# Three scalings on GpSimd, and latent attention's entrance, copies and end rearranged

## The reference

```python
# layer 0: differential attention, per block of 128 queries
p = softmax(where(causal, q @ k.T * scale, NEG_INF))      # two maps, c = 0 and 1
a = p[:, :, 0] - lam * p[:, :, 1]
o = rms_norm(a @ v, subln) * (1.0 - lambda_init)          # per head, width 128
y = o.reshape(B, S, H * 2 * dh) @ w_o
# layer 1: latent attention
lat = h @ w_in                                            # 384 + 256 + 32 columns
q = (rms_norm(cq) @ w_uq); kv = (rms_norm(ckv) @ w_ukv)   # normalised per head, rotated
p = softmax(where(causal, s, NEG_INF))
y = (p @ v).reshape(B, S, H * MLA_V) @ w_o
```

## Time and profile before

| | us |
|---|---|
| runs shown | 1137.25, 1137.52, 1135.13 (median 1137.25) |
| profiled execution: its own time | 1136.97 |
| its span, first to last instruction | 1135.2 |
| PE busy | 1043.2 (92%) |
| DVE busy | 608.2 (54%) |
| ACT busy | 329.0 (29%) |
| POOL busy | 92.1 (8%) |

### The profile page before, as it was taken

How to read it: one execution, slowest core, us unless ns; L and a number is a source line. 1 busy time by engine, 2 the same in 40 slices (tenths; PEclk the granted TensorE clock), 3 DMA queues, 4 the chain that set the end, 5 groups by cost and what they waited for, 6 DMA issues and landing times.

```text
span 1135.2 us, 15295 instructions
## 1 busy us (share of the span) xinstructions
PE 1043.2 (92%) x5662; PEld 633.0 (56%) x5662; DVE 608.2 (54%) x1460; ACT 329.0 (29%) x896; POOL 92.1 (8%) x129
## 2 busy tenths in 40 slices
PE   4999999999998999897889999999998999979996
PEld 3444444656466666564556556655456656646652
DVE  6899989898646322221246577766235622222224
ACT  4321112875131111111124545666122121111110
POOL 1000000000011111111000000000000111201200
PEclk9999999999999999999999999999998999999999
DMA  9929868928568999999996300401826899999998
GB/s 368 405 79 392 332 259 328 420 83 347 190 270 340 409 417 419 418 418 420 417 396 261 124 1 38 149 1 61 334 88 259 311 420 420 418 414 418 419 416 351
DMA packets 66814, 341.44 MB, mean 301 GB/s; under 512 B 11110, under 2 KB 11366, under 8 KB 36400
## 3 DMA queue, kind: packets, MB, share of 16 engines
q1 hardware_dynamic: 49952, 297.68, 64.8%
q0 software_dynamic: 15120, 37.63, 8.5%
q10 hardware_dynamic: 1664, 5.09, 1.1%
HBM read 320.90 MB, written 37.24 MB: 315 GB/s over the span
## 4 chain that ended last, share of the span: by engine, by line
PE 75%; DMA 8%; SPq 5%; DVE 5%; ACT 3%; issue 3%; DVEq 0%; ACTq 0%; POOLq 0%
PE PP L928 16%; PE PP L694 12%; PE PP L804 10%; PE PP L943 8%; PE PP L716 3%; SPq L531 3%; DMA AHS<-in_moe_w 3%; PE PP L1145 3%; PE PP L667 2%; PE PP L1111 2%; PE PP L1149 2%; PE PP L901 2%; PE PP L753 2%; SPq L547 2%; PE PP L764 2%
## 5 line engine op out<-in xcount | busy, mean ns | idle before, releaser
L694 PE MATMUL PP<-ring,AHS 128*128 128x512 f32 x320 | 139.9, 592 | 0.0
L2028 DVE TENSOR_TENSOR PS<-PS,PP 128x256 f32<-128x256 f32 x33 | 13.9, 421 | 195.9 <-PE PP L928 186.3
L804 PE MATMUL PP<-ring,AHS 128*128 128x512 f32 x256 | 111.4, 593 | 0.8 <-ACT AHS L1491 0.8
L2035 DVE SCALAR_TENSOR_TENSOR PS<-PP,small,GF 128x512 f32<-128x512 f32 x66 | 46.5, 746 | 111.3 <-PE PP L943 100.7
L694 PEld LDWEIGHTS PP<-ring,AHS 128*128 128x128 f32 x320 | 59.7, 190 | 69.8 <-issue 69.8
L928 PE MATMUL PP<-RQK,RV 128*64 128x256 f32 x640 | 75.2, 392 | 10.5 <-issue 8.4
L804 PEld LDWEIGHTS PP<-ring,AHS 128*128 128x128 f32 x256 | 48.0, 190 | 58.4 <-issue 58.4
L928 PE MATMUL PP<-ring,RV 128*64 128x256 f32 (+1 forms) x608 | 75.5, 389 | 4.3 <-ACT RV L1525 1.7
L1549 ACT ACTIVATE PS<-PP 128x256 f32<-128x256 f32 x33 | 12.7, 384 | 217.1 <-PE PP L928 151.1
L928 PEld LDWEIGHTS PP<-RQK,RV 128*64 128x64 f32 x640 | 56.4, 142 | 32.1 <-issue 17.7
L928 PE MATMUL PP<-AHS,RV 128*64 128x256 f32 x640 | 71.9, 380 | 2.1 <-issue 2.1
(11 more groups left out here) (351 smaller groups left out, 1675.4 us busy)
## 6 DMA issues: line engine op xcount, KB each, us to landing
AHS<-in_moe_w SPq DMA_DIRECT2D x61, 1024.0 KB
ring<-in_moe_w SPq DMA_DIRECT2D x58, 1024.0 KB, 21.2
RQK<-in_moe_w SPq DMA_DIRECT2D x52, 1024.0 KB
ring<-in_ada_t SPq DMA_DIRECT2D x22, 1024.0 KB, 19.9
AHS<-in_ada_t SPq DMA_DIRECT2D x18, 1024.0 KB
X<-in_moe_w SPq DMA_DIRECT2D x16, 1024.0 KB, 23.3
ring<-in_da_w_qkv SPq DMA_DIRECT2D x10, 1024.0 KB, 13.8
RQK<-in_ada_t SPq DMA_DIRECT2D x8, 1024.0 KB
```

The source lines that it names most:

```text
L694: last = mm(PB[qkv_bank(n)][:, :], HT[:, c, t * P:(t + 1) * P], us[c // 4][:, (c % 4) * NH:(c % 4 + 1) * NH], start=c == 0, stop=c == C - 1)
L804: last = mm(PB[2 * t + n][:, :], (OT, OTM)[l][:, k, t * P:(t + 1) * P], us[k // 2][:, (k % 2) * D + n * NH:(k % 2) * D + (n + 1) * NH], st ...
L2035: last = stt(ysb[b][:, cols], PB[5 + m][:, :], weight, GF[:, cols], ALU.mult, ALU.mult)
```

## The change

1. Differential attention: `SCALED` is gone. The outputs of tiles 0, 1 and 2 are scaled by GpSimd, in its program behind the zero fill of y_d and the load of a row. Tile 3 stays with VectorE, which first waits for GpSimd's three.
2. Latent attention: the copy of a tile 0 (both heads) goes from ScalarE to VectorE.
3. Entrance: the scores of steps 0 and 1 are made in banks 6 and 7 behind projection 14, with maxima, exponentials and normalisation beside projection 15. The last two transposes of queries and keys use banks 6 and 7. Of the last but one ScalarE copies both. Three groups of fillers (6 + 3 + 8 calls) are left out. The probabilities lie in other places.
4. End: for tile 0, chunks 0 to 2 of the first half of the output projection are put before the transposes of steps 29 and 31 and after the latter, and four more chunks and seven of the second half behind the values of pair 7.

```diff
-def mla_on_vector(i):
+def by_vector_alone(i):
+    return i % T == 0
+def by_both(i):
     return i % T >= 2
...
-        prm = [view(PS, 1024 * b, 2, S) for b in range(3)] + [view(RA, 2560 + T * ROPE, 2, S)]
+        prm = [view(PS, 2048, 2, S), view(RA, 2560 + T * ROPE, 2, S), view(PS, 1024, 2, S), view(PS, 0, 2, S)]
+        prm_first = view(RA, 2560 + T * ROPE + 2 * S, 2, P)
...
@@ tensor, project_out
-                        begun = 1 if (l, t, n) == (0, 0, 0) else 0
+                        begun = 0 if t else C - 1 if l else 1 - n
@@ tensor, mla
+                def scores_ahead(t):
+                    for a in range(2):
+                        o = early_scores(t, a)
+                        mm(o, mq[0][0:QK, a, t * P:(t + 1) * P], mk[0][0:QK, a, 0:(t + 1) * P], start=True, stop=False)
+                        last = mm(o[:, t * P:(t + 1) * P], identb[:, :], maskb[:, :], start=False, stop=True)
+                    last.then_inc(sem("sc"), 1)
...
                     if i >= T:
                         mla_values(i // T - 1, i % T)
+                    if i == 29:
+                        pe.wait_ge(sem("exp"), 32 + 31)
+                        mixed(1, 0, 0, wo, (0,))
+                    if i == 31:
+                        mixed(1, 0, 0, wo, (1,))
                     mla_turn(i)
...
                     if n >= 2:
                         turn_qk(n - 2)
-                first_scores(0)
-                keep_busy(7, 6)
-                turn_qk(4 * T - 2)
-                first_scores(1)
-                turn_qk(4 * T - 1)
-                keep_busy(7, 3)
-                pe.wait_ge(sem("mtev"), 4 * T)
-                pe.wait_ge(sem("mtevD"), 4 * T)
-                for i in range(32):
+                    if n == 4 * T - 2:
+                        scores_ahead(0)
+                        scores_ahead(1)
+                pe.wait_ge(sem("exp"), 32 + 2)
+                turn_qk(4 * T - 2, 6)
+                scores_behind_projection(2, 4 * T - 2)
+                pe.wait_ge(sem("mtev"), 4 * T - 2)
+                pe.wait_ge(sem("mtevD"), 4 * T - 2)
+                attend(0)
+                scores_behind_projection(3, 4 * T - 1)
+                pe.wait_ge(sem("mtev"), 4 * T - 1)
+                turn_qk(4 * T - 1, 6)
+                attend(1)
+                for i in range(2, 32):
...
-                    if i == 2:
-                        keep_busy(7, 8)
-                    if i:
+                    if i > 2:
                         attend(i - 1)
                 attend(31)
+                mixed(1, 0, 0, wo, (2,))
                 for k in range(T):
                     mla_values(7, k)
+                mixed(1, 0, 0, wo, (3, 4, 5))
+                pe.wait_ge(sem("omla"), 7)
+                mixed(1, 0, 0, wo, (6,))
+                mixed(1, 0, 1, wo, range(C - 1))
@@ scalar, mla
+                    if n == 4 * T - 1:
+                        queries_out(n - 2)
                     roots(n)
-                    if n >= 2:
+                    if 2 <= n < 4 * T - 1:
                         queries_out(n - 2)
+                    if n == 4 * T - 2:
+                        exps(1, 0, 0)
+                        exps(1, 1, 1)
                 queries_out(4 * T - 2)
-                exps(1, 0, 0)
+                exps(1, 2, 0)
                 queries_out(4 * T - 1)
-                exps(1, 1, 1)
+                exps(1, 3, 1)
@@ vector, da_attention and output_norm
-                    if i in SCALED:
-                        output_scaled(*SCALED[i])
...
+                dve.wait_ge(sem("on"), T - 1)
                 for half in range(2):
                     output_scaled(T - 1, half)
@@ vector, mla
+                    if by_vector_alone(i):
+                        v.tensor_copy(turned_pair(t), PP[2][:, :, 0:(t + 1) * P].rearrange("p a (k q) -> p a k q", k=t + 1)).then_inc(
                             sem("tev1"), 1)
...
+                    if n == 4 * T - 2:
+                        maxima(1, 0, 0)
+                        maxima(1, 1, 1)
                     heads(n)
-                keys_out(4 * T - 2)
-                maxima(1, 0, 0)
-                keys_out(4 * T - 1)
-                maxima(1, 1, 1)
-                for i in range(32):
+                    if n == 4 * T - 2:
+                        normalise(0)
+                        normalise(1)
+                maxima(1, 2, 0)
+                probabilities_out(0)
+                maxima(1, 3, 1)
+                for i in range(2, 32):
                     normalise(i)
+                    if i == 2:
+                        keys_out(4 * T - 1)
@@ gpsimd, layer 0, behind gate_row(0, 1)
+                    for t in range(T - 1):
+                        pool.wait_ge(sem("osd"), t + 1)
+                        for half in range(2):
+                            ot = OTOK[:, t, half * NH:(half + 1) * NH].rearrange("p (h x) -> p h x", h=4)
+                            factor = hrs[:, 0, 8 * t + 4 * half:8 * t + 4 * half + 4].unsqueeze(2).broadcast_to([P, 4, P])
+                            last = g.tensor_tensor(ot, ot, factor, ALU.mult)
+                        last.then_inc(sem("on"), 1)
```

More of the change, by code:

```diff
@@ L126, with vector_copies, scalar_copies @@
 SUMS = {17: (0, 0), 18: (0, 1), 19: (1, 0), 20: (1, 1), 25: (2, 0), 26: (2, 1)}
-SCALED = {21: (0, 0), 22: (0, 1), 23: (1, 0), 24: (1, 1), 29: (2, 0), 30: (2, 1)}
 ROOTS = {20: 0, 22: 1, 28: 2}
-def mla_on_vector(i):
+def by_vector_alone(i):
+    return i % T == 0
+def by_both(i):
     return i % T >= 2
-def mla_copies(i):
-    return sum(mla_on_vector(j) for j in range(i + 1))
+def vector_copies(i):
+    return sum(by_vector_alone(j) or by_both(j) for j in range(i + 1))
+def scalar_copies(i):
+    return sum(not by_vector_alone(j) for j in range(i + 1))
 def wait(eng, sem, value):
@@ L1151, in project, with turn_qk, scores_behind_projection @@
                     last.then_inc(sem("mla_kv"), 1)
[L1153 removed]
+                def turn_qk(n, bank=4):
                     pe.wait_ge(sem("my"), n + 1)
[L1156 to L1157 removed]
+                    if bank == 4:
+                        wait(pe, sem("mtev"), n)
+                        wait(pe, sem("mtevD"), n)
                     for m, y in enumerate((QY, KY)):
                         for h in range(4):
[L1160 removed]
+                            last = nc.tensor.transpose(PB[bank + m][0:QK, h * P:(h + 1) * P], y[n % 2][:, h, :], ident[:, :])
                     last.then_inc(sem("mt"), 1)
[L1163 to L1165 removed]
+                def scores_ahead(t):
[4 more added lines that the diff above has]
+                    last.then_inc(sem("sc"), 1)
+                def scores_behind_projection(i, n):
                     for name in ("msq", "mev"):
                         pe.wait_ge(sem(name), n + 1)
[L1168 to L1171, removed]
+                    scores(1, i, i % 2)
                 def attend(i):
@@ L1184, in mla @@
                         turn_qk(n - 2)
-                first_scores(0)
-                keep_busy(7, 6)
-                turn_qk(4 * T - 2)
-                first_scores(1)
-                turn_qk(4 * T - 1)
-                keep_busy(7, 3)
-                pe.wait_ge(sem("mtev"), 4 * T)
-                pe.wait_ge(sem("mtevD"), 4 * T)
-                for i in range(32):
+                    if n == 4 * T - 2:
[12 more added lines that the diff above has]
+                for i in range(2, 32):
+                    if i == 5:
+                        pe.wait_ge(sem("mtev"), 4 * T)
+                        pe.wait_ge(sem("mtevD"), 4 * T - 1)
+                    if i == 30:
+                        wo = [take(1, "wo", u) for u in range(4)]
+                        pe.wait_ge(sem("omla"), 6)
                     if i + 2 < 32:
@@ L1348, in exps @@
                     total = ls[:, b, a:a + 1] if l or a else l1[:, DA_H * t + g:DA_H * t + g + 1]
-                    last = fn(dst[:, a, 0:L], PB[2 * pair + a][:, 0:L], ACT.Exp, bias=nmx[:, b, a:a + 1], accum_out=total)
+                    dst = probabilities(i, a) if l else pr[b][:, a, 0:L]
+                    src = early_scores(i, a) if l and i < 2 else PB[2 * pair + a][:, 0:L]
+                    last = fn(dst, src, ACT.Exp, bias=nmx[:, b, a:a + 1], accum_out=total)
                 last.then_inc(sem("exp"), 1)
@@ L1773, in maxima @@
                 wait(dve, sem("exp"), n - 1)
-                red(nmx[:, b], PP[pair][:, :, 0:L], AX.X, ALU.max, negate=True).then_inc(sem("nm"), 1)
+                o = PP[pair][:, :, 0:L]
+                if l and i < 2:
+                    o = PB[6 + i][:, 0:2 * L].rearrange("p (a n) -> p a n", a=2)
+                red(nmx[:, b], o, AX.X, ALU.max, negate=True).then_inc(sem("nm"), 1)
             def da_attention():
```

50 lines of the change are left out of this document (31 added, 19 removed).

## The result

The changed kernel takes 1127.14 us (median of 4 runs, 1126.80 to 1128.31), the one before 1136.97 on the same chip (4 runs, 1135.13 to 1137.52): a ratio of 0.9926 [0.9902, 0.9951]. Forecast were 1128.0 and 1125.8 to 1132.5. The profiled execution took 1127.12, its span is 1125.4. A repeat of both kernels on another chip (last experiment) gave 1128.73 against 1134.40, a ratio of 0.9951 [0.9937, 0.9964]: a gain of 5.7 us there, in place of 9.8 here.

The account below looks back on a forecast made before the run. TensorE was taken to bound three quarters of the chain, with DMA and its queue most of the rest. The terms 0.4 + 2.3 + 3.6 + 2.9 = 9.2 us off gave 1128.0 us, range 1125.8 to 1132.5.

Parts of the forecast that it names:

- What bounds it, and gains pass one to one: Whole kernel: three quarters of the chain is TensorE, and attention ending N us earlier makes the end N us earlier.
- Rival C: Start of layer 1's stream: bound to something that doesn't move, so only 0.4 us stays, 1136.8; chance 0.03.
- Part 1: Differential attention: moving scaling from VectorE to GpSimd gains 0.4 us, between +1.0 and -1.7.
- the choice between the bounds: Differential attention: GpSimd slows VectorE not at all, or VectorE stands for each of four multiplies; 0.4 us gain taken.
- the 1.3 I put in: Differential attention: assumed length in us of one GpSimd 128x512 multiply, the middle of 0.3 and 2.3.
- rival B: Differential attention, steps 21 to 25: L1785 stands behind GpSimd's multiplies, costing 1.0 to 1.7 us, 1129.8; chance 0.12.
- The 0.8 that I gave to an undisturbed VectorE: Differential attention, transposes of steps 22 to 25: gains of 0.27, 0.40 and 0.12 us without VectorE's scaling, together 0.8.
- Part 2: Latent attention's steady groups: tile 0's copy on VectorE removes six gaps of 0.39 us before tile 1's transposes, 2.3 us.
- Part 3: Latent attention's entrance: the reordered schedule starts scores 7 3.7 us earlier; 3.6 us taken, between 1.5 and 4.4.
- Rival A: Latent attention's entrance: without fillers, idle pieces and short transposes let the clock fall, costing 3.5 us, 1131.5; chance 0.11.
- Rival D: Latent attention: clock stays at 1.2 GHz throughout; 15 us of full-clock work affected give 1143; chance 0.04.
- Part 4: End of latent attention: output-projection chunks fill TensorE's idle places, gaining 2.9 us, from below 1.5.

Follow-up runs that it names:

- The delay of 8.04 us: 36 matmul calls whose result nobody reads, put ahead of latent attention's output projection in the changed kernel: 1134.72 us (12 runs).
- the pieces: The changed kernel with each 128x512 multiply of GpSimd cut into four of 128x128, one for each head: 1126.41 us, ratio 0.9927.

## Why the prediction was right, and which step was not

- **What bounds it, and gains pass one to one:** right, within what was measured. The delay of 8.04 us came through as 7.1 in the medians, give or take 2 to 3, and the stages show 7.4 of it ahead of the experts and none returned behind. Rival C (1136.8) is refuted. What the prediction lacked is that an edit can change a stage far behind it (below).
- **Part 1, "I take a gain of 0.4":** wrong in sign, -0.2 measured. Two steps failed. The first is the choice between the bounds: the rival's mechanism is real. L1785's successor stood until the end of the running multiplies in two of the five steps, 0.74 and 0.75 us each. By the Trainium skill (SBUF — State Buffer, "SBUF: two separate sides"), where of a VectorE operation with two SBUF inputs and a GpSimd one that reads SBUF the later waits for the whole of the earlier, this is what had to come, and the traces agree (1.36 and 1.50 us in place of 0.62 and 0.75, and 1.49 in place of 1.04 for the multiply that came second). I had named that rule and weighed it with half, where the row that it spoke of was the very operation that the transposes wait for. The second is the price: a multiply takes 1.02, not the 1.3 I put in, and only two pairs collided with the critical operation where the stage waits for it, so the loss was 0.2 and not the 1.0 to 1.7 of rival B. (The third pair held L1843 for 0.82 us too, at 259.87, but TensorE's steps behind step 25 are not longer for it.) The 0.8 that I gave to an undisturbed VectorE was too low: the pieces show 1.16 in those steps and 1.44 in the stage, and with the multiplies moved away the same steps lose 1.16 as well.
- **Part 2, 2.3:** measured 2.56, a group 10.32 us where 10.36 was forecast. The handovers of 0.04 around the gap went as well. The copy of tile 1 was indeed next and didn't wait: 61.92 of 61.92.
- **Part 3, 3.6:** measured 3.41, of which 0.44 is the removed wait of part 2 in this place. The order laid out by hand was right to 0.12 at the last scores (3.58 against 3.7). The prediction didn't say that part 3 gives nothing without part 2 (+0.53 alone, -2.97 behind it), though its own schedule had VectorE's copy in it.
- **Rival A, the clock at the entrance:** it did not decide here (1.00 in 22.08 us), but its reason holds. Where TensorE stood 2.47 or 2.08 us at this place the clock fell, and once it fell with the unchanged 1.11 and 0.31. A chance of 0.11 for it fits one of seven profiles, as far as seven can say; the price was 1.7 us there and not 3.5. Rival D found no sign: where the clock had fallen in this entrance, the next scores of 512 columns, 3.4 us later, took their 1.88 again.
- **Part 4, 2.9:** measured 2.97, with chunks in the three places forecast. The number holds the 0.94 that part 2 takes by itself: behind parts 2 and 3 the filled end adds 2.00. Parts 2 and 4 were booked right in sum and not each.
- **Sum:** the parts make 0.2 - 2.56 - 3.41 - 2.97 = -8.74 against -9.2. The rest of the -9.85 between the two profiled executions is in stages with no edit in them, -1.08, +0.14, -1.96, -0.14 and +1.95 (the last 0.02 are rounding). The forecast's 1128.0 is so close to 1127.14 because the parts gave 0.46 less than forecast, and the others, each up to 2 us, happened to sum up to 1.09 more. That is luck, and the repeat shows it: there the gain is 5.7 us [4.1, 7.1], which doesn't reach the forecast 9.2, though both profiles of the kernel after have the same edited stages. The kernel before took 1134.13 to 1135.34 (medians) on the three chips of the experiments, 1.6 to 2.8 us less than in the first comparison. So the edited stages bear the prediction out, and the whole gain only in part.

**The stage that grew.** Before, TensorE runs at 0.93 in the 50 us of layer 1's experts from 985.90, and at 0.86 in the matching 50 us of the kernel after. The chain of the kernel after has one long row there, behind the tile of leftover tokens:
```profile
1008.48 6.45 issue
1014.93 6.16 PE PP L946 x33
```
The kernel before has 0.65 us at this place:
```profile
1020.55 0.65 issue
1021.20 8.81 PE PP L928 x64
```
Eight of the fourteen profiles have 6.25 to 7.8 us here, six have 0.65. Those with the long wait take 249.85 to 253.8 us from the first expert step to the end (the median of the eight is 251.4), those with the short one 248.6 to 250.1 (249.6). Both profiles of the kernel after have the long one, but so has the kernel of before without fillers, and the kernel with pieces and fillers has the short one.

It is no chance, though: it goes with the number of matmuls in TensorE's program. The page of each of the eight profiles with the long wait counts 5628 of them, those of the other six 5638, 5662 or 5700. Two pairs of kernels differ by fillers of the entrance alone, some 290 us ahead (in the second pair a semaphore wait comes with them). The kernel before has the 0.65 above; without its 17 fillers it has
```profile
1019.07 6.25 issue
```
and its experts of layer 1 take 249.85 us in place of 249.31. The kernel with the multiplies in pieces has
```profile
1007.44 6.27 issue
```
and with five fillers added it has
```profile
1007.95 0.65 issue
```
with 249.92 us in place of 251.32. So part 3, which leaves out 17 fillers, brought the long wait into the kernel after. In the 20 us from the wait's begin the granted clock is 0.74 in the kernel after, against 0.91 before; in the second pair it is 0.83 with the long wait and 1.00 with the short. The two pairs put 0.5 and 1.4 us of the +1.95 down to it. The kernel with part 1 taken out has the long wait too and takes 250.00, so what makes the rest stays open.

The DMA view shows what arrives in the wait. This is its line for 1012.1 to 1013.4 in the kernel after (packets, MB, share):
```profile
q8 instruction: 1, 0.02, 5.3%
```
The kernel before has no such line in its wait, 1019.1 to 1021.2. The packet lands at 1013.30, and TensorE goes on at 1014.93. All eight long waits have one such packet of 16 KB in them that lands 1.6 to 1.7 us before TensorE goes on; none of the six short ones has one. At the matching place of layer 0, also behind the conditional block of the leftover tokens, all fourteen profiles have a wait of 3.6 to 3.9 us, again with a packet that lands 1.6 to 1.7 us before its end. The plainest reading is that TensorE waits for its own next instructions, and that the number of instructions ahead decides whether they are there; no experiment moved the packet by itself, so this stays a reading.

## What to carry to other kernels

Before work goes from VectorE to GpSimd, look at what VectorE runs at that time: if it is an operation with two SBUF inputs on the critical path, price it as standing to the end of the GpSimd instruction, and cut GpSimd's work into pieces that are shorter than VectorE's slack (here 0.40 in place of 1.02, a stage of 63.8 us in place of 65.4). An entrance or an end can be scheduled by hand from rows to a tenth of a microsecond, but an edit that moves an order may need another edit to pay, so run the parts alone and together. Fillers and other edits that change the number of an engine's instructions can lengthen a wait behind a conditional block far away (here 0.65 to 6.25 us): look at that wait before and after. Judge terms below 0.2% by the length of their own stage, since here unedited stages moved by up to 2 us between programs.

## What the hardware showed beyond that

- GpSimd's multiply of 128x512 by a broadcast factor took 1.02 us, of 128x128 0.40; VectorE's of 128x512 took 0.68. Beside GpSimd even a VectorE operation on 128x1 took up to 0.88 in place of 0.22.
- GpSimd is held in the same way: a 128x512 multiply issued while VectorE's L1843 ran took 1.49 us in place of 1.04, and a 128x128 one 0.71 to 0.85 in place of 0.40.
- After TensorE had stood 2.47, 2.08 or 2.11 us between short matmuls, its granted clock fell to the 1.2 GHz level, in the first two by the end of the wait (four transposes took 1.09 in place of 0.63), in the third 1.2 us later. The same entrance with waits of 1.11 and 0.31 kept 2.4 GHz in six profiles and lost it in one.
- Behind a conditional block TensorE stood 0.65 us or 6.25 to 7.8, by the number of matmuls in its program, with a packet of a queue named `instruction` landing 1.6 to 1.7 us before the end of each long wait.
